# Gate tiles of the merge stage: two plain products per body against a 2x2 block product of seven half-size ones

## The reference, cut to what matters

```python
proj = jnp.einsum('bsd,de->bse', h, w_in[l])
q, k, v, z_a, u_b, v_b, z_b, g_a, g_b = jnp.split(proj, pts, axis=-1)
y_a = stick_breaking_attention(q, k, v) * silu(z_a)        # 512 wide
y_b = spatial_gating(gelu(u_b), gelu(v_b), ...) * silu(z_b)  # 512 wide
p_a = jnp.einsum('bse,ed->bsd', y_a, w_up_a[l])
p_b = jnp.einsum('bse,ed->bsd', y_b, w_up_b[l])
merged = jax.nn.sigmoid(g_a) * p_a + jax.nn.sigmoid(g_b) * p_b
x = x + jnp.einsum('bsd,de->bse', merged, w_out[l])
```

## Time and profile before

| | |
|---|---|
| median of 3 runs | 1763.36 us (1763.0 to 1763.55) |
| span of the profiled execution | 1764.2 us |
| TensorE busy (matmuls) | 1743.4 us, 99% |
| VectorE busy | 1125.2 us, 64% |
| ScalarE busy | 860.2 us, 49% |
| GpSimd busy | 38.8 us, 2% |
| sgu body 1 to body 2 (mixing to mixing) | 1547.67 to 1566.18 us |
| out stage begins | 1709.85 us |
| HBM traffic | 92 GB/s over the span |

### The profile page before, as it was taken

The page is one execution under the profiler, slowest core; times in us unless marked ns, Lnnn a source line. Parts: engine busy times, 40 slices in busy tenths (PEclk is TensorE's granted clock), DMA queues, the critical chain, the costliest instruction groups (busy, mean ns, idle before and its releaser), DMA issues.

```text
span 1764.2 us, 25427 instructions
## 1 busy us (share of the span) xinstructions
PE 1743.4 (99%) x9092; PEld 1365.3 (77%) x9092; DVE 1125.2 (64%) x1847; ACT 860.2 (49%) x1360; POOL 38.8 (2%) x71
## 2 busy tenths in 40 slices
PE   9999999999999999999999999999999999999998
PEld 6777777778888888788887788888887766677887
DVE  7788888567777733467776677777433555665445
ACT  6565666444444422367776444444332466643222
POOL 2000000000000000000000000000000000000000
PEclk9999999999999999999999999999999999999999
DMA  5522221133222322233331333232321312323322
GB/s 185 176 84 73 72 67 54 49 120 95 92 89 92 117 99 82 84 114 112 104 102 61 107 95 95 95 94 96 106 97 52 108 36 72 101 72 103 98 87 70
DMA packets 45817, 163.53 MB, mean 93 GB/s; under 512 B 5825, under 2 KB 8148, under 8 KB 45744
## 3 DMA queue, kind: packets, MB, share of 16 engines
q1 hardware_dynamic: 40848, 148.00, 25.9%
q0 software_dynamic: 4464, 14.47, 2.8%
q10 hardware_dynamic: 432, 0.07, 0.0%
HBM read 155.89 MB, written 6.63 MB: 92 GB/s over the span
## 4 chain that ended last, share of the span: by engine, by line
PE 92%; DVE 3%; ACT 3%; issue 2%; DMA 0%; POOL 0%; SPq 0%; DVEq 0%; ACTq 0%
PE acc L618 23%; PE acc L619 23%; PE acc L620 23%; PE acc L644 9%; PE pa L618 1%; PE pa L619 1%; PE pa L620 1%; PE pbc L1078 1%; PE pbc L1003 1%; ACT wsplit L1219 1%; PE pa L1066 1%; PE pa L747 1%; PE pd L1091 1%; PE pd L1016 1%; PE pd L1015 0%
## 5 line engine op out<-in xcount | busy, mean ns | idle before, releaser
L618 PE MATMUL acc<-xhi,wsplit 128*128 128x512 f32 x1200 | 487.5, 406 | 1.1 <-DVE at_vs L2223 1.0
L1219 ACT ACTIVATE wsplit<-wraw 128x1024 fp32r<-128x1024 f32 (+1 forms) x250 | 274.1, 1098 | 439.7 <-PE acc L620 400.8
L619 PE MATMUL acc<-xlo,wsplit 128*128 128x512 f32 x1200 | 475.5, 396 | 0.0
L620 PE MATMUL acc<-xhi,wsplit 128*128 128x512 f32 x1200 | 475.5, 396 | 0.0
L1777 DVE TENSOR_TENSOR wsplit<-wraw,wsplit 128x1024 fp32r<-128x1024 f32 (+1 forms) x247 | 314.4, 1274 | 142.0 <-ACT wsplit L1219 141.1
L618 PEld LDWEIGHTS acc<-xhi,wsplit 128*128 128x128 f32 x1200 | 226.0, 188 | 68.5 <-issue 14.0
L620 PEld LDWEIGHTS acc<-xhi,wsplit 128*128 128x128 f32 x1200 | 225.9, 188 | 54.7
L619 PEld LDWEIGHTS acc<-xlo,wsplit 128*128 128x128 f32 x1200 | 226.4, 189 | 51.4 <-issue 1.4
L644 PE MATMUL acc<-xhi,wsplit 128*128 128x512 f32 x464 | 159.1, 415 | 0.2 <-DVE wsplit L1777 0.2
L620 PE MATMUL acc<-hid_hi,wsplit 128*128 128x512 f32 x352 | 139.6, 396 | 0.0
L619 PE MATMUL acc<-hid_lo,wsplit 128*128 128x512 f32 x352 | 139.5, 396 | 0.0
(11 more groups left out here) (417 smaller groups left out, 2493.0 us busy)
## 6 DMA issues: line engine op xcount, KB each, us to landing
wraw<-w SPq DMA_DIRECT2D x220, 512.0 KB, 3.5
wraw<-w SPq DMA_DIRECT2D x32, 704.0 KB, 4.1
bias_dram<-ext_dram POOLq DMA_DIRECT2D x1, 4096.0 KB, 21.8
bias<-bias_dram POOLq DMA_DIRECT2D x16, 256.0 KB, 3.0
at_ks<-at_ks SPq DMA_DIRECT2D x16, 256.0 KB, 2.9
crow<-row_dram POOLq DMA_DIRECT2D x8, 256.0 KB, 3.7
brow<-row_dram POOLq DMA_DIRECT2D x8, 256.0 KB, 4.3
h<-xT SPq DMA_DIRECT2D x3, 512.0 KB, 8.4
```

What stands on the lines that cost most here:

```text
L618: mm(out, whi[:, k, :], a[:, x_at + k, :], start=(k == first), stop=False)
L619: mm(out, whi[:, k, :], b[:, x_at + k, :], start=False, stop=False)
L620: m = mm(out, wlo[:, k, :], a[:, x_at + k, :], start=False, stop=(k == last))
L1219: A(split(s, i, j, 0), raw(s, j), ACT.Copy).then_inc(w_hi_ready, 1)
```

## The change

The two gate tiles of a merge body are taken as one product of a 2x2 block matrix (rows: `g_a` tile, `g_b` tile; columns: the two halves of the contraction, 4 blocks of 128 each) with a 2x2 block matrix of the activations (the halves of the contraction by the halves of the 512 positions). Such a product can be made from seven products of half-size blocks instead of eight, with sums of blocks on both sides:

- Activations: sums t1, t2, t3, t4 of quarters of `xhi`+`xlo` are made once. VectorE makes them in ten operations of 1024 elements (`turn`), ScalarE casts each, VectorE makes four low parts (`turn_low`). These lie in the VectorE order of sgu bodies 0 (five turns), 1 (a low part, two turns), 2 (a low part, three turns) and 3 (two low parts), ahead of what reads `mixed` in bodies 0 to 2. t1 takes the place of the quarter x12.
- Weights: a body has seven forms of 4 blocks: a11, a12, a22 as loaded, and s1, s2, s3, s4 as sums. s1 and s3 are made by transfers: SyncE loads a base of 256 KB, and GpSimd's queue adds another 256 KB onto it (`accum_op=add`). s2 and s4 are made by VectorE, of 512 elements each. With ua and ub (the halves of the `w_up` tile) that is nine forms of 512 elements per body, each with its own cast and low part, in a ring of six.
- TensorE: seven products of 12 matmuls of 256 columns, and ua and ub as before with 12 of 512 columns. They write to six half banks, of which `bank_64` serves both s2 and a22 in one body. In the last body of sgu the first six forms of body 0 stand before the mixing, where two full tiles stood.
- Afterwards: ScalarE copies one product (`copy_p`), VectorE makes u, w, v and the four quarters of the result (`mid_u`, `mid_w`, `c22`, `c11`, `c12`, `c21`) by seven operations of 256 elements, and multiplies by `rstd` as before.
- Order: the merge stage is written out without a loop; all its steps count on two semaphores, `merge_dve` and `merge_act`, by tables (`merge_counts`); forms used by TensorE count on `form_used`. The first cast and low part of the out stage move into the last body of merge, and so does the second one.

The core of the diff:

```diff
+FORMS = ("a11", "s2", "a12", "s1", "s3", "s4", "ua", "a22", "ub")
+RING = 6
...
+                    for b in range(s.bodies - 1):
+                        sp.wait_ge(ev("merge_dve"), MERGE_DVE["low", form(b, "s3")])
+                        load_bases(b + 1)
+                        if b + 2 < s.bodies:
+                            sp.wait_ge(ev("merge_dve"), MERGE_DVE["low", form(b, "a22")])
+                            load_gb(b + 2)
+                        sp.wait_ge(ev("merge_dve"), MERGE_DVE["low", form(b, "ub")])
+                        load_up(b + 1)
+                        if b + 2 < s.bodies:
+                            sp.wait_ge(ev("merge_dve"), MERGE_DVE["s4", b + 1])
+                            load_ga(b + 2)
...
+                def sums(b):
+                    pool.wait_ge(ev("bases_landed"), 32 * b + 32)
+                    pool.dma_start(form_raw(form(b, "s1")), w8[m.src + 3 * b + 1, :, 512:1024], accum_op=ALU.add
+                                   ).then_inc(ev("sums_landed"), 16)
+                    pool.dma_start(form_raw(form(b, "s3")), w8[m.src + 3 * b + 1, :, 0:512], accum_op=ALU.add
+                                   ).then_inc(ev("sums_landed"), 16)
...
                     if last:
-                        tile(st["merge"], 0, 0)
-                        tile(st["merge"], 0, 1)
+                        for name in FORMS[0:6]:
+                            merge_step(0, name)
...
+            def merge_step(b, name):
+                n = form(b, name)
+                out, x = {"a11": (bank_1, x11), "s2": (bank_64, xt2), "a12": (bank_2, x21), "s1": (bank_5, xt1), "s3": (bank_7, xt3),
+                          "s4": (bank_3, x22), "ua": (bank_ua, None), "a22": (bank_64, xt4), "ub": (bank_ub, None)}[name]
...
+                pe.wait_ge(ev("merge_dve"), MERGE_DVE["low", n])
+                if b == 0:
+                    if name == "a12":
+                        pe.wait_ge(ev("mixed_read"), GPP)
...
+                elif name == "s2":
+                    pe.wait_ge(ev("merge_dve"), MERGE_DVE["c21", b - 1])
...
+                for k in range(4):
+                    mm(out, whi[:, k, :], x[0][:, k, :], start=(k == 0), stop=False)
+                    mm(out, whi[:, k, :], x[1][:, k, :], start=False, stop=False)
+                    m = mm(out, wlo[:, k, :], x[0][:, k, :], start=False, stop=(k == 3))
+                m.then_inc(ev("form_used"), 1)
...
+                    if i == 0:
+                        turn(0, t1_raw, x11[0], x12[0], ALU.subtract)
+                        turn(1, t1_raw, t1_raw, x11[1], ALU.add)
+                        turn(2, t1_raw, t1_raw, x12[1], ALU.subtract)
+                        turn(3, t_raw, t1_raw, x22[0], ALU.add)
+                        turn(4, t_raw, t_raw, x22[1], ALU.add)
+                    if i == 1:
+                        turn_low(t_raw, xt2, "t2")
+                        turn(5, t_raw, x21[0], t_raw, ALU.subtract, ("turn_low", "t2"))
+                        turn(6, t_raw, t_raw, x21[1], ALU.add)
+                    if i == 2:
+                        sums_low(0)
+                        low_form(0)
...
+                        sums_high(0)
+                        turn_low(t_raw, xt4, "t4")
+                        turn(7, t_raw, x12[0], x22[0], ALU.subtract, ("turn_low", "t4"))
...
+                for b in range(KD):
+                    for k in range(len(FORMS)):
+                        n = b * len(FORMS) + k + RING - 1
+                        more = n < MERGES and n >= 9
+                        if k == 0 and b > 0:
+                            low_form(n)
+                            merged(b - 1)
+                        elif k == 2 and b > 0:
+                            mid_u(b)
+                            merged_low(b - 1)
+                        elif k == 3 and b > 0:
+                            c11(b)
+                        elif k == 4 and b > 0:
+                            mid_w(b)
+                        elif k == 5:
+                            if b > 0:
+                                c22(b)
+                            if b + 1 < KD:
+                                sums_low(b + 1)
+                        elif k == 6:
+                            c12(b)
+                        elif k == 8:
+                            c21(b)
+                        if more and k > 0:
+                            low_form(n)
+                        if k == 7 and b + 1 < KD:
+                            sums_high(b + 1)
```

More of the change, by code:

```diff
@@ L116, in plan @@
         stages[name] = Stage(n, bodies, kc, slots, first, list(landed), src[which])
+        if name == "merge":
+            src[which] += n * bodies
+            landed = [c + l for c, l in zip(landed, (bodies, bodies, bodies // 2, bodies // 2))]
+            continue
         first += n * bodies
@@ L369, in build @@
         for name, after in zip(stages, stages[1:]):
-            if st[name].slots == st[after].slots or st[name] in rolling:
+            if after != "merge" and (st[name].slots == st[after].slots or st[name] in rolling):
                 st[name].follow = st[after]
@@ L599, in weights_of @@
                                           ).then_inc(ev("wcur_ready"), 1)
+                m = st["merge"]
+                def sums(b):
[4 more added lines that the diff above has]
+                                   ).then_inc(ev("sums_landed"), 16)
                 weights_of(0)
-                with pool.Fori(1, GPP) as i:
+                with pool.Fori(1, GPP - 1) as i:
                     pool.wait_ge(ev("mixed"), i)
                     weights_of(i)
+                sums(0)
+                pool.wait_ge(ev("mixed"), GPP - 1)
+                weights_of(GPP - 1)
+                for b in range(1, KD):
+                    sums(b)
         @block.tensor
@@ L1147, in _ @@
+            def merge():
+                for b in range(KD):
+                    for name in FORMS[6 if b == 0 else 0:]:
+                        merge_step(b, name)
             n = 1
@@ L1689, in merge, with gate, merged_hi @@
             def merge():
-                s = st["merge"]
                 tables("sigmoid_and_others")
[L1693 to L1707, removed]
+                o = st["out"]
+                def gate(b, j):
+                    act.wait_ge(ev("merge_dve"), MERGE_DVE[f"g{j}", b])
+                    A(ga[:, j, :], ga[:, j, :], ACT.Sigmoid).then_inc(ev("merge_act"), 1)
+                def merged_hi(b):
+                    act.wait_ge(ev("merge_dve"), MERGE_DVE["mg", b])
+                    A(mg_hi[:, b, :], mg[:, 0, :], ACT.Copy).then_inc(ev("merge_act"), 1)
+                for b in range(KD):
+                    for k in range(len(FORMS)):
+                        n = b * len(FORMS) + k + RING - 1
+                        if n < MERGES and n >= 9:
+                            cast_form(n)
+                        if k == 0 and b > 0:
+                            copy_p(b)
+                        if k == 2 and b > 0:
+                            merged_hi(b - 1)
+                        if k == 6:
+                            gate(b, 0)
+                        if k == 8:
+                            gate(b, 1)
+                        if b == KD - 1 and k == 5:
+                            act.wait_ge(ev("form_used"), form(b, "s3") + 1)
+                            cast(o, 0, 0)
+                        if b == KD - 1 and k == 7:
+                            act.wait_ge(ev("form_used"), form(b, "a22") + 1)
+                            cast(o, 0, 1)
+                merged_hi(KD - 1)
             n = 1
```

304 lines of the change are left out of this document (252 added, 52 removed).

## The result

The changed kernel takes 1810.47 us (median of 5 runs, 1807.12 to 1813.49), the kernel before 1763.55 in the same comparison (1763.0 to 1765.89): 1.026 of its time, 95% interval [1.0247, 1.0272], 47 us slower. The forecast was 1769.4, its range 1762 to 1784.

A forecast was written before the change was run, and what follows sets the result against it. The prediction took TensorE, busy 99%, as the bound: 11.2 us gained in merge, 15.4 lost at the start (+4.2), plus 1.8 charged for VectorE, makes 6.0 more. Forecast 1769.4 us, range 1762 to 1784.

The forecast's parts named there:

- the transfers' term: Merge bodies: two plain copies and two adding ones take 8.1 us, hidden behind VectorE's own work within 0.2.
- upper end: Merge transfers, highest estimate: 3.5 for plain copies, 0.6 between issues, 7 for the adding pair, 11 us in all.
- Rival A: Merge: adding transfers make the sums late and set the loop; 1781 us at 10 us, 1788 at 11; chance 0.25.
- an estimate of 0.5 more than plain: Merge adding transfers: 256 KB behave as 512 because two sources are read, 0.5 us more than plain.
- The start: Gating bodies to merge body 1: TensorE waits on VectorE's order, 15.4 us lost against 11.2 gained.
- second mixing: Gating stage: a low part and two activation sums on VectorE delay this TensorE step, 1.4 us lost.
- the walk: Gating bodies followed in VectorE's code order by operation durations, to find TensorE's waits: 15.4 us lost.
- The gain of 1.40 a body: Merge, TensorE: half-width products shorten a body from 16.88 to 15.48 us, 11.2 over eight bodies.
- Rival C: Merge, TensorE: 256-column matmuls don't hold 0.1173 us, say 0.134; the gain vanishes, 1777 us; chance 0.03.
- VectorE's 15.3 of 15.48: Steady merge body: VectorE's work of 13.1 us plus round trips through ScalarE; TensorE sets the pace, 0.2 in hand.
- The charge of 0.3 in each of six bodies: Merge bodies after the second: allowance for VectorE's narrow slack against TensorE, 1.8 us in all.
- Rival B: Gating: the start's waits are covered and stay under 11.2 us; 1758.6 us; chance 0.10.

The follow-up runs named there:

- the last kernel: Against the doubled-area kernel with early first sums: activation sums spread over VectorE's idle places, then the last gating body reordered; 1761.11 us, 0.9987 of the kernel before.

## Why the prediction was wrong

**The step that failed is the transfers' term: 8.1 us, free within 0.2.** It took 15.5 in the body shown. The plain copies were put at 3.5, after a weight load of 512 KB in one piece; they took 6.3 from the low part's end to GpSimd's first issue. The adding pair was put at 4.6 (0.6 + 4), nearest the plain rows of GpSimd's queue; it took 9.25. Two things were missed. First, the pairs alone already take 4.0 and 6.25, 10.3 in all, as body 1 shows: near my upper end of 11. Second, the other 5.2 us come in the bodies in which the stage's own loads of 512 KB are in flight beside them, one beside the copies and two beside the adding pair. Rival A names these loads, and I set a mean DMA share of 0.3 against them; in the stretch that counted it was 0.88 and then 1.02. That the loads are the reason is read from the bodies of one run, with none, one and two of them beside the pair; no run moved them.

The upper end is also added up wrongly. "The pair's 4.3 and as much again" is 8.6, and I wrote 7; with 8.6 it would have been 12.7, and rival A's time at that end about 1800, which is above my range as well.

With 15.5 the prediction's own sentence, "each us beyond costs one in each body", gives 7.4 us, and the five middle bodies (23.41, 23.38, 21.30, 23.19, 23.06) are 7.4 above 15.47 in the mean. The loop adds up the same way: 15.5 of transfers and 7.4 of VectorE are 22.9, the mean of the five. The mechanism, rival A, was right; its price was set for 10 or 11 us, and so its time was 1781 to 1788, and not 1810.

The Trainium skill (Collectives: The Full Stack, Part 3, "The bandwidth ceiling") says that the add of a ReduceScatter reads two sources; the prediction made of it an estimate of 0.5 more than plain. By the DMA engines' time the trace agrees with a factor near two: the adding pair for body 1, alone, holds them at 0.55 for 6.3 us, the same pair without adding at 0.43 for 3.6 (1592.9 to 1596.5), 2.2 times as much. The latency that I made of it was too small: 6.25 against 3.7 for these two pairs, and 9.25 against 5.6 beside two weight loads.

**The start: the sum came out by luck, the parts did not.** Forecast 15.4 lost. In the run without adding the stretch to the out stage is 4.7 longer with 11.2 gained, so 15.9 were lost (16.5 by the medians, 5.3 apart). By the waits of that run: first mixing 2.4 (forecast 2.6), second mixing none (1.4), a12 1.4 (1.5), s1 3.3 (3.6), last mixing 3.0 (3.1), body 1 on c21 1.6 (2.9), ua 0.2 (0.5). These make 11.9. Another 3.4 lie in the granted clock, which the walk left at 1.00: the windows 1550 to 1555 and 1595 to 1600 of that run, behind the first and the last mixing, have 0.66, which is 1.7 us less work in each; 0.6 I can't place. So the total agreed by two errors against each other: the waits were put some 4 too high, 2.7 of it at the second mixing and body 1, and the clock 3.4 too low.

**One wait was not in the walk.** The s2 sum of body 0 waits for the first adding transfers, which start only when the last low part of the gating stage has freed their areas: base copies at 1562.37, adding ones at 1567.07, the sum at 1575.20. Four weight loads of 512 KB are issued from 1563.23 to 1564.65, beside them. I followed the loop in the merge and did not follow its first turn. It costs 4.2 us before the last transposes, and with the clock behind it `ua` of body 0 comes 4.7 later than in the run without adding.

**Right.** The gain of 1.40 a body: 256-column matmuls start 0.117 apart in the full windows, and bodies of 15.46 to 15.47 stand against 15.48 forecast. Rival C falls with it. VectorE's 15.3 of 15.48 is confirmed by the run with two more sums. The charge of 0.3 in each of six bodies (1.8 in all) was not needed: with 0.2 in hand nothing was lost. With s1 and s3 loaded whole the time is 1768.8, against a forecast of 1769.4 with free transfers, but this too is in part luck: the 1.8 too much for the merge hides about 1.1 too little for the start. Rival B, the start covered, was false for this order; the last kernel, at 1761.1, comes near it by another order.

**Open.** No run moved the weight loads away from the adding pair, so how much of the 47 us that alone would give back is not known. Why an adding pair takes 6.25 us alone, at a DMA share of only 0.55, is not settled. The 2.4 us of s3 on t3 were not followed further.

## What to carry to other kernels

A transfer that reads and writes the area that the consumer must first release closes a loop: price the loop from the release to the next use, in pairs, with each handover between queues and beside the loads that will be in flight then, and not by the median of one transfer. A mean DMA share of a body (0.3 before, 0.5 after) says little about the 9 us in which a pair is waited for. Give such an area a second copy before anything is done about the transfer itself. Where new work goes to an engine that has 36% idle, what counts is its place in the order: the same arithmetic took 1770.0 us in one order and 1761.1 in another.

## What the runs showed of the hardware

An adding transfer of 256 KB lands 7.3 us after its issue in the median of 16 (plain, same queue and place: 4.0), from 3.7 to 9.3 by what else is in flight. The two issues of a pair are 0.84 and 1.18 us long in place of 0.54 and 0.54; the second starts 0.54 after the first in both kernels. The trace also shows more and smaller packets. GpSimd's queue in the kernel after and in the run with plain transfers (packets, MB, share of 16 engines):

```profile
q0 software_dynamic: 6768, 18.66, 4.2%
```
```profile
q0 software_dynamic: 5744, 18.66, 3.5%
```

The same bytes take 1024 more packets, 64 for each of the 16 adding transfers.

TensorE's granted clock fell behind most of its waits of over 2 us: from 1500 to 1750 the ten profiles have 32 such waits, and 27 have a granted clock of 0.50 beside or behind them, all nine of 4 us and more among these. The PE timeline of the kernel after, behind a wait for c21:

```profile
1656.38 0.55 PE L1294 MATMUL acc<-xt_hi,wsplit 128*128 128x256 f32 x1 [5.43 <-DVE ga L2738]
1656.73 0.41 PE L1295 MATMUL acc<-xt_lo,wsplit 128*128 128x256 f32 x1
...
1661.00 0.35 PE L1294 MATMUL pbc<-xhi,wsplit 128*128 128x256 f32 x1
1661.19 0.28 PE L1295 MATMUL pbc<-xlo,wsplit 128*128 128x256 f32 x1
1661.31 0.29 PE L1296 MATMUL pbc<-xhi,wsplit 128*128 128x256 f32 x1
```

The starts are 0.213 apart for 21 matmuls, at a granted clock of 0.50 (1.2 GHz), and then 0.12 again, at 1.00 (2.4 GHz): 21 x 0.096 = 2.0 us on top of the 5.43 waited. Behind a wait of 2.86 (at 1610.40) it was 13 matmuls, some 1.2 us. Such stretches are what lowers the granted clock to 0.83 in the merge windows above. Not every wait does it. In the run without the adding, s1 waited 3.32 and went on at full rate:

```profile
1586.19 0.35 PE L1290 MATMUL pa<-xhi,wsplit 128*128 128x256 f32 x1 [3.32 <-DVE xlo L2679]
1586.39 0.28 PE L1291 MATMUL pa<-xlo,wsplit 128*128 128x256 f32 x1
```

while 2.38 before its first mixing and 3.00 before its last were followed by the half clock, and so was the same wait of 3.32 for s1 in the kernel after (at 1589.80). What tells these cases apart was not tested.
